# The last residual quarter of the gate takes a trip through DRAM, and table steps in linear attention stand together

## What is computed

```python
h = h + swiglu(rms_norm(h, norm_ffn[i]), ffn_w_in[i], ffn_w_out[i])
gate = jax.nn.sigmoid(rms_norm(h, ple_norm[i]) @ ple_w_gate[i])
h = h + gate * (p[i] @ ple_w_proj[i])
...
la_f = heads(jax.nn.log_sigmoid((zf @ w_gate_f + b_gate_f).astype(F32)) / GLA_TAU, GLA_HK)
b = jnp.cumsum(log_a.astype(F32).reshape(bsz, nh, n, c, dk), axis=3)
q_in = qf * jnp.exp(b)
```

## Time and profile before

| what | us |
|---|---|
| median of 3 runs | 898.44 |
| lowest, highest | 898.26, 900.61 |
| the profiled execution | 898.33 |
| its span, first to last instruction | 896.7 |
| PE busy in the span | 891.8 |
| DVE busy | 652.4 |
| ACT busy | 504.8 |

### The profile page before, as it was taken

The page is one execution under the profiler, slowest core; times in us unless marked ns, Lnnn a source line. Parts: engine busy times, 40 slices in busy tenths (PEclk is TensorE's granted clock), DMA queues, the critical chain, the costliest instruction groups (busy, mean ns, idle before and its releaser), DMA issues.

```text
span 896.7 us, 12085 instructions
## 1 busy us (share of the span) xinstructions
PE 891.8 (99%) x4364; PEld 737.2 (82%) x4364; DVE 652.4 (73%) x985; ACT 504.8 (56%) x820; POOL 68.9 (8%) x88
## 2 busy tenths in 40 slices
PE   9999999999999999999999999999999999999998
PEld 8988888888888888778888888888888888887777
DVE  6985478677747488997786777655779987779763
ACT  6756555444444576888564444434665445577581
POOL 0001000000000303211100000000010000215200
PEclk9999999999999999999999999999999999999999
DMA  7953548766667476433187676757377773767501
GB/s 263 337 181 118 164 153 308 259 243 243 247 238 250 126 264 220 149 118 116 65 306 250 234 257 242 266 180 248 113 299 252 263 272 136 262 216 249 183 29 48
DMA packets 76995, 187.56 MB, mean 209 GB/s; under 512 B 6852, under 2 KB 31812, under 8 KB 76936
## 3 DMA queue, kind: packets, MB, share of 16 engines
q1 hardware_dynamic: 75480, 182.99, 58.6%
q0 software_dynamic: 1024, 3.15, 1.0%
q10 hardware_dynamic: 432, 0.66, 0.2%
HBM read 171.83 MB, written 14.94 MB: 208 GB/s over the span
## 4 chain that ended last, share of the span: by engine, by line
PE 99%; DMA 1%; ACT 0%; issue 0%; DVE 0%
PE bank L1773 87%; PE bank L1811 3%; PE bank L1826 1%; PE bank L2077 1%; PE bank L2103 1%; PE bank L2182 1%; PE bank L2212 1%; DMA h<-x_dram 1%; PE bank L2088 0%; PE bank L1933 0%; PE bank L2168 0%; PE bank L1985 0%; PE bank L1981 0%; PE bank L2063 0%; PE bank L2192 0%; PE bank L1792 0%
## 5 line engine op out<-in xcount | busy, mean ns | idle before, releaser
L1074 DVE TENSOR_TENSOR wlo<-raw,whi 128x1024 fp32r<-128x1024 f32 x295 | 347.0, 1215 | 43.1 <-ACT whi L679 42.5
L679 ACT ACTIVATE whi<-raw 128x1024 fp32r<-128x1024 f32 x295 | 304.3, 1061 | 131.0 <-PE bank L1773 107.9
L1773 PE MATMUL bank<-whi,x_hi 128*128 128x512 f32 x560 | 152.4, 394 | 0.0
L1773 PE MATMUL bank<-wlo,x_hi 128*128 128x512 f32 x560 | 149.8, 389 | 0.0
L1773 PE MATMUL bank<-whi,x_lo 128*128 128x512 f32 x560 | 149.7, 389 | 0.0
L1773 PEld LDWEIGHTS bank<-wlo,x_hi 128*128 128x128 f32 x560 | 105.1, 188 | 22.2
L1773 PEld LDWEIGHTS bank<-whi,x_lo 128*128 128x128 f32 x560 | 105.1, 188 | 21.9
L1773 PEld LDWEIGHTS bank<-whi,x_hi 128*128 128x128 f32 x560 | 103.5, 188 | 22.2 <-issue 1.8
L1773 PE MATMUL bank<-whi,y_hi 128*128 128x512 f32 x396 | 107.7, 394 | 0.1
L1773 PE MATMUL bank<-wlo,y_hi 128*128 128x512 f32 x396 | 106.0, 389 | 0.0
L1773 PE MATMUL bank<-whi,y_lo 128*128 128x512 f32 x396 | 106.0, 389 | 0.0
(11 more groups left out here) (252 smaller groups left out, 897.1 us busy)
## 6 DMA issues: line engine op xcount, KB each, us to landing
raw<-stream_dram SPq DMA_DIRECT2D x295, 512.0 KB, 4.8
ffn_blocks<-ffn_blk SPq DMA_DIRECT2D x22, 256.0 KB, 2.2
ffn_land<-ffn_blocks SPq DMA_DIRECT2D x22, 256.0 KB, 4.3
second_blocks<-h_blk SPq DMA_DIRECT2D x8, 256.0 KB, 2.0
h_land<-second_blocks SPq DMA_DIRECT2D x8, 256.0 KB, 3.2
cv_blocks<-cv_blk SPq DMA_DIRECT2D x7, 256.0 KB, 2.3
cv_land<-cv_blocks SPq DMA_DIRECT2D x7, 256.0 KB, 3.4
h_blocks<-h_blk SPq DMA_DIRECT2D x3, 512.0 KB, 3.1
```

The lines of the kernel that those rows point to most:

```text
L679: A(whi[:, u % RING, :], raw[:, u % SLOTS, :], ACT.Copy).then_inc(sem("w_hi"), 1)
L1074: V.tensor_tensor(wlo[:, u % SLOTS, :], raw[:, u % SLOTS, :], whi[:, u % RING, :].bitcast(F32), ALU.subtract).then_inc(sem("w_lo"), 1)
L1773: last = T.matmul(bank[pair + t][:, :], lhs[a][:, kt, t * P:(t + 1) * P], w[:, place(w, u), kk * NW:(kk + 1) * NW], start=part != 1 and k ...
```

## The change

**Tables.** In linear attention `expabs` and `ln` on ScalarE both stand at 5 (6 and 7 before), and VectorE's `gates` and `ln` at 4 and 5 (5 and 7 before). In differential attention VectorE's second `more` and first `unit` stand at 8 and 9 (10 and 10 before).

```diff
-        (6, "expabs", 0), (7, "ln", 0), (9, "cumulate", 0), (10, "cumulate", 1), (13, "tile", 3), (17, "cross", 0),
+        (5, "expabs", 0), (5, "ln", 0), (9, "cumulate", 0), (10, "cumulate", 1), (13, "tile", 3), (17, "cross", 0),
...
-        (4, "zT", 0), (4, "tile", 1), (5, "z4", 0), (5, "gates", 0), (7, "ln", 0), (9, "tile", 2),
+        (4, "zT", 0), (4, "tile", 1), (5, "z4", 0), (4, "gates", 0), (5, "ln", 0), (9, "tile", 2),
...
-        (5, "rope", 0), (6, "more", 0), (6, "sums", 0), (8, "rope", 1), (8, "sums", 1), (10, "more", 1),
-        (10, "unit", 1), (11, "sums", 2), (11, "rope", 2), (11, "more", 2), (11, "scores", 0), (12, "scores", 1),
+        (5, "rope", 0), (6, "more", 0), (6, "sums", 0), (8, "rope", 1), (8, "sums", 1), (8, "more", 1),
+        (9, "unit", 1), (11, "sums", 2), (11, "rope", 2), (11, "more", 2), (11, "scores", 0), (12, "scores", 1),
```

```diff
+PIECES = ("mix0 q0", "mix0 q1", "ple0 q1", "gate0 t0", "gate0 t1", "mix1 q0", "mix1 q1", "ple1 q1", "gate1 t0", "gate1 t1",
+          "cv q0", "cv q1", "mb q0", "mb q1")
+GATE_ORDER = ((0, 0), (0, 1), (1, 0), (0, 2), (0, 3))
...
+            for tile in (PLE0, PLE1):
+                for n, (t, k) in enumerate(GATE_ORDER):
+                    SOURCE[END[tile] + n] = END[tile + t] + k
...
-                at = END[tile + 1] + 10
+                at = END[tile + 1] + 12
...
-            def second_blocks(r, tile):
-
-                at = END[tile] + (7 if tile == CV_IN else 8)
+            def trips(at, *names):
+
                 fetch(done, at)
...
+                for name in names:
+                    n, q = piece(name), slot(name)
+                    sp.wait_ge(sem("g_blk"), n + 1)
+                    sp.dma_start(s_dram[n], sblk[:, q, :]).then_inc(sem(f"g_out{q}"), 16)
+                for name in names:
+                    n, q = piece(name), slot(name)
+                    sp.wait_ge(sem(f"g_out{q}"), 16 * turn(name))
+                    sp.dma_start(sland[:, q, :, :], s_dram[n].rearrange("q n -> (q n)")
                                  .rearrange("(i p w) -> p i w", i=P // B, p=P)).then_inc(sem(f"g_land{q}"), 16)
...
-                done = second_blocks(2 * n, tin)
+                done = trips(END[tin] + 11, f"mix{n} q0", f"mix{n} q1")
...
-                done = gate_blocks(n, tin + FT + 2)
-            done = second_blocks(4, CV_IN)
-            fetch(done, done_at(CV_IN) + 10)
+                done = trips(END[tin + FT + 2] + 11, f"ple{n} q1")
+                done = trips(END[tin + FT + 4] + 11, f"gate{n} t0", f"gate{n} t1")
+            done = trips(END[CV_IN] + 10, "cv q0", "cv q1")
+            fetch(done, done_at(CV_IN) + 13)
...
-                fetch(at + 1, done_at(CV_IN + t + 1) + 10)
-            done = END[CV_IN + 8] + 10
+                fetch(at + 1, done_at(CV_IN + t + 1) + 13)
+            done = END[CV_IN + 8] + 13
...
-            done = second_blocks(5, MB_IN)
+            done = trips(END[MB_IN] + 11, "mb q0", "mb q1")
```

```diff
-                lhs_hi(src, norm_gain(j), (6, 7))
+                lhs_hi(src, norm_gain(j), (6,))
                 squares(j, 1)
+                split_to(END[tple] + 8)
+                pair_hi(j, src, f"ple{n} q1", 6)
+                A(spare[:, n:n + 1], cols[:, 0:1], ACT.Sigmoid)
                 act.wait_ge(sem("rstd"), j + 1)
                 for half in range(2):
                     t = tple + 2 * half
-                    split_to(END[t + 1] + AHEAD - 2 * half)
-                    c.wait(act, "w_used", END[t + 1])
+                    over = END[t + 1 + (half == 0)]
+                    split_to(over + AHEAD - 1 - half)
+                    c.wait(act, "w_used", over)
...
-                        A(sig[:, k, :], bank[2 * (t % 2) + k][:, :], ACT.Sigmoid, scale=rstd[:, j, k:k + 1])\
+                        A(sig[:, k, :], bank[(4 if half else 2 * (t % 2)) + k][:, :], ACT.Sigmoid, scale=rstd[:, j, k:k + 1])\
                             .then_inc(sem("ple_sig"), 1)
...
-                residual(tout + 1, 1)
+                split_to(END[tout + 2] + AHEAD - 2)
+                c.wait(dve, "w_used", END[tout + 2])
+                for lo in (HALF // 2, 0):
+                    for t in range(TT):
+                        V.tensor_tensor(h[:, t, HALF + lo:HALF + lo + HALF // 2], h[:, t, HALF + lo:HALF + lo + HALF // 2],
+                                        bank[2 * ((tout + 1) % 2) + t][:, lo:lo + HALF // 2], ALU.add)\
+                            .then_inc(sem("h_part" if lo else "h_new"), 1)
+                    if lo:
+                        dve.wait_ge(sem("h_part"), TT * (n + 1))
+                        pair_blk(f"ple{n} q1", 0, 6, False)
                 split_to(END[tout + 2] + 1 + AHEAD)
-                lhs_lo(src, norm_gain(j), (6, 7))
+                lhs_lo(src, norm_gain(j), (6,))
+                split_to(END[tple] + 8)
+                pair_lo(j, src, f"ple{n} q1", 6)
...
-                    dve.wait_ge(sem("ple_sig"), TT * (2 * n + half + 1))
                     c.wait(dve, "w_used", END[t + 2])
                     for k in range(TT):
+                        dve.wait_ge(sem("ple_sig"), TT * (2 * n + half) + k + 1)
```

```diff
+                pair = 2 * (tile % 2) if pair is None else pair
...
-                more2 = list(half0) + [None, None]
-
-                def second_half2():
-                    more2[2:4] = h_T(1, 3 * n + 2)
-
-                product(tple, src, "ple_sig", need=more2, hooks=[(1, second_half2)])
-                product(tple + 1, PT, "ple_gated", need=[("pT", 2 * (n + 1))])
+                more2 = list(half0) + [None, piece_need(f"ple{n} q1")]
+                for at, (t, k) in enumerate(GATE_ORDER):
+                    if at == 2:
+                        pe.wait_ge(sem("h_new"), 4 * (3 * n + 1) + 4)
+                        more2[2:3] = lhs_T(h, (6,))
+                    product(tple + t, PT if t else src, "ple_gated" if t else "ple_sig" if k == 3 else None,
+                            need=[("pT", 2 * (n + 1))] if t else more2, only=k, at=END[tple] + at)
                 half1 = []
-                product(tple + 2, src, "ple_sig")
-                half1 += [("g_lhs", 2 * (2 * n + 1) + k + 1, ("g_hi", 4 * (2 * n + 1) + k + 3)) for k in range(2)]
+                product(tple + 2, src, "ple_sig", pair=4)
+                r = piece(f"gate{n} t0")
+                half1 += [("g_lhs", r + k + 1, ("g_hi", 2 * r + k + 3)) for k in range(2)]
                 product(tple + 3, PT, "ple_gated")
                 c.up("h_new", 4)
                 return half1
```

More of the change, by code:

```diff
@@ L77, with piece, slot, turn @@
 LAST = ((0, 0, NW), (1, 0, NW // 2), (1, NW // 2, NW))
+PIECES = ("mix0 q0", "mix0 q1", "ple0 q1", "gate0 t0", "gate0 t1", "mix1 q0", "mix1 q1", "ple1 q1", "gate1 t0", "gate1 t1",
+          "cv q0", "cv q1", "mb q0", "mb q1")
+GATE_ORDER = ((0, 0), (0, 1), (1, 0), (0, 2), (0, 3))
 PAIR_ORDER = ((0, 0), (0, 1), (1, 0), (1, 1), (0, 2), (0, 3), (1, 2), (1, 3))
+def piece(name):
+    return PIECES.index(name)
+def slot(name):
+    return int(name[-1])
+def turn(name):
+    return sum(slot(other) == slot(name) for other in PIECES[:piece(name) + 1])
 def done_at(tile):
@@ L1118, in second_lo, with pair_blk @@
-            def second_lo(j, dst, r, base):
+            def pair_blk(name, news, kt0, first):
+                for t in range(TT):
+                    if first:
+                        dve.wait_ge(sem("h_new"), news + t + 1)
+                    at = slice(kt0 * P, (kt0 + 2) * P)
+                    last = V.transpose(sblk[:, slot(name), :].rearrange("p (f k t b) -> p t f k b", f=P // B, k=2, t=TT)[:, t],
+                                       h[:, t, at].rearrange("p (k b f) -> p f k b", b=B, f=P // B))
+                last.then_inc(sem("g_blk"), 1)
@@ new lines, in pair_lo @@
+            def pair_lo(j, dst, name, kt0):
+                n = piece(name)
+                for k in range(2):
+                    kt = kt0 + k
+                    dve.wait_ge(sem("g_hi"), 2 * n + k + 1)
+                    for t in range(TT):
+                        at = slice(t * P, (t + 1) * P)
+                        part = sland[:, slot(name), :, :].rearrange("p i (k t b) -> p k t i b", k=2, t=TT)[:, k, t]
+                        last = V.scalar_tensor_tensor(dst[1][:, kt, at].rearrange("p (i b) -> p i b", b=B), part,
+                                                      norm_gain(j)(kt),
+                                                      dst[0][:, kt, at].bitcast(F32).rearrange("p (i b) -> p i b", b=B),
+                                                      ALU.mult, ALU.subtract)
+                last.then_inc(sem("g_lhs"), 1)
@@ L1725, in product @@
             def product(tile, lhs, signal, kt0=0, need=None, hooks=(), beside=None, part=None,
-                        only=None, at=None, turned=False, inside=None):
-                pair = 2 * (tile % 2)
+                        only=None, at=None, turned=False, inside=None, pair=None):
```

(7 more changed lines are left out.)

105 lines of the change are left out of this document (36 added, 69 removed).

## The result

The changed kernel takes **899.89 us** (median of 21 runs, 899.32 to 902.0), the kernel before beside it 898.75 (21 runs, 898.26 to 900.71): a ratio of **1.0016, 95% interval 1.001 to 1.0022**, which is 0.9 to 2.0 us. The medians differ by 1.14 us. Runs of either kernel lie in two groups about 2 us apart (16 and 5 of the 21 before, 14 and 7 after); the lower groups differ by 1.0 us. The forecast was 898.8, 0.45 us above the kernel before: the time lies in its range, but the loss is more than twice what was forecast.

What follows compares the result with a forecast made beforehand. TensorE was taken as the bound, busy 891.8 us with 99% of the last chain on it. From 898.33, less 0.84 at the gates, plus 1.29 in linear attention: 898.8 us, range 897.2 to 900.0 (chance 0.90).

Steps and rivals of the forecast that it cites:

- Four transposes fewer: Gates on TensorE: four transposes less save 0.42 us a gate, 0.84 for two.
- the transposes might have run for nothing: Rival at the gates: transposes run in room TensorE has anyway and return nothing, 899.6 us; chance 0.06.
- The new trip: Gate: the quarter leaving TensorE goes through DRAM and back; no cost, its high part 1.2 us early.
- a late trip: Rival at the gate's last unit: landing after 310.1 holds TensorE 2.1 us at each gate, 903.0 us; chance 0.07.
- Table ahead and fresh banks: Gate: sigmoid's table loaded earlier, second gate tile in other banks; no cost, TensorE not waiting for a sigmoid.
- SP: SP's order: trips three loads back; no cost and no gain, as TensorE had no wait on loads.
- Differential attention's steps: VectorE's two moved steps in differential attention: no cost, more than the 0.5 us of slack.
- Linear attention's tables: Moved VectorE and ScalarE steps before the first scores: a loss of 1.29 us, bounds 0 and 2.35.
- a drain of 1.38 us: Rival in linear attention: ScalarE's table switch also costs its drain, loss 2.2, 899.7 us; chance 0.02.
- term 2: The gate's new trip through DRAM: no cost if it is in time, with 2.8 us of room to land.
- term 3: Gate: sigmoid's table ahead and the second gate tile in other banks, no cost.
- term 4: SP's trips three loads back: no cost, nothing gained.

Runs made afterwards that it cites:

- trip_slow: Kernel with gate and SP changed and the old tables, SP writing the gate's new piece to DRAM three times before reading it back: 900.41 us.
- bank_old: Kernel with gate and SP changed and the old tables, the second gate tile put back into the first one's banks: 901.89 us.
- sp_back: Kernel with gate and SP changed and the old tables, every trip three loads further forward in SP's order, as before the change: 898.50 us.
- df_back: The changed kernel with differential attention's VectorE table as before, all else still changed: 899.81 us.
- pad_before: Kernel before plus six do-nothing memsets on VectorE, into a new tile, and four fulfilled waits on SP: 902.39 us.
- gate_pads: Kernel with gate and SP changed and the old tables, plus six memsets into a new tile and eight fulfilled waits on SP: 901.61 us.
- best: gate_pads with retuned tables: linear attention with one unit less ahead of the running sums, differential attention's fourth tile one unit earlier: 900.94 us.
- pad_back: Kernel before plus seven memsets on VectorE into an existing tile, so no tile moves, and six fulfilled waits on SP: 899.31 us, ratio 1.0012.
- best2: best with the six memsets put into an existing tile, so that no tile moves: 897.47 us, ratio 0.9989 to the kernel before.

## Why the prediction had the sign right and the sum short

Forecast +0.45 us (-0.84 and +1.29). The parts of the two traces give +1.30 at the scores, -0.56 in the middle and +0.33 at the end, +1.07; the medians differ by 1.14.

1. **Four transposes fewer** (forecast -0.42 a gate): measured -0.40 and -0.40, in the shift of the matmuls across each gate. Right. The Trainium skill (Perfetto Trace Analysis, section Identifying the Most-Contended Engine) judges TensorE's headroom by the busy share of weight loads, among others; at 82% there would have been room, in which the transposes might have run for nothing. The trace does not agree: nearly all of the 0.42 came back.
2. **The new trip**: no wait; copies 1.34 us early, forecast 1.2. trip_slow confirms the room and that a late trip stays local. Yet the trip had a cost of another kind, below.
3. **Table ahead and fresh banks**: no wait; bank_old gives the cost of leaving the banks out, 3.36 us.
4. **SP**: sp_back shows nothing either way.
5. **Differential attention's steps**: no cost, as forecast. The wait that appeared in that stage is there with the old table as well (df_back).
6. **Linear attention's tables** (forecast +1.29): +1.30 and +1.31. The chain came out step by step: 47.60 less the start's 0.53 is 47.07, forecast 47.04. Line 1966's loads start 1.31 later, but most of the wait stands one step ahead. Line 1958's loads need both directions too, and wait for VectorE's last copy of decays, which ends at 54.93 now, 0.05 us before they start, and ended 0.27 us before them in the kernel before (53.08 and 53.35). So the 0.35 us there, which the prediction read as a wait on VectorE, held 0.27 us of slack. Here the Trainium skill (ScalarE: Activation LUTs, section What ACT_TABLE_LOAD costs) would have added a drain of 1.38 us to the table switch; in the changed kernel the load begins at 43.65 and the Exps at 44.95, 1.30 later, so again none is seen.

**The step that failed** is "no cost" of term 2, the new trip. It weighed the trip's arrival, but not that the trip's added instructions move the programs themselves; the fresh banks of term 3 and the order of term 4 are not the source, as bank_old and sp_back, which undo them, keep both costs. Six places further on, VectorE's stall of 0.27 us falls between two short instructions with nothing in hand, where TensorE has no slack, and costs it 0.29 us; SP's last code load falls among the output's packets, for 0.33. Together that is 0.62 us, the part of the loss that the sum lacks. No row ahead of the prediction showed such a stall, but a bound of zero had no row behind it either: the price named for term 2 was that of a late trip alone.

What stays open: what sets the start's 0.76 us; why VectorE stands still at that one place (the crossing is inferred); why the kernel before ends at 3.08 us and others without a load among the output at 2.92 to 2.95; and which address the weights of a matmul want (only one shift of 32 bytes was tried).

## What to carry to other kernels

Joining steps on a full chain gains only if fewer units stand ahead of its end: Ln came 1 us earlier and lost 2.35 to two units moved behind it, while one unit less ahead of the sums won 0.26. Where a change is worth half a microsecond, look in the trace for idle times that no semaphore explains, and test them by instructions that do nothing, put into memory that is there already. Compare by parts of the span: the start's scatter alone was as large as any term here.

## What the hardware showed

- **A tile 32 bytes further on slowed matmuls that take it as weights** from 226.7 to 233.3 ns, 3.5 us over the kernel (pad_before, gate_pads, best); back at 226.7 when the tiles lay as before (pad_back, best2). It was seen for `mid_hi` and `mid_lo`.
- **A place in a program can cost 0.27 us** on VectorE between short instructions (eight runs), and nothing behind a running reduction of 0.7 us (pad_before).
- **Code loads share the DMA engines with data:** with one of 8 KB (0.32 us on one engine, 0.62 in pad_back) among the last output packets the kernel ended 0.3 to 0.4 us later than before.
